# A two-layer decoder trunk on one core: TensorE turns the activations before its last half of a sum, small fp32 products sit in tiles of the array, and ScalarE scales the probabilities

## What is computed

```python
def reference(x, ...):
    for l in range(DEPTH):                       # 2
        x = layer_norm(ALPHA * x + 0.5 * swiglu(x, ffn1_w_gate[l], ffn1_w_up[l], ffn1_w_down[l]), ...)
        mix = hybrid_mixer(x, w_in[l], ...)
        x = layer_norm(ALPHA * x + mix, ln2_g[l], ln2_b[l])
        x = layer_norm(ALPHA * x + 0.5 * swiglu(x, ffn2_w_gate[l], ffn2_w_up[l], ffn2_w_down[l]), ...)

def hybrid_mixer(x, w_in, ...):
    proj = x @ w_in                              # 4864 columns
    b_g, c_g, h, u, q, k, v, gates = split(proj)
    y_conv = short_conv_mixer(b_g, c_g, h, ...) @ w_br_conv
    y_ssm  = s5_mixer(u, ...) @ w_br_ssm         # 16 groups of 16 channels, 64 complex states each
    y_attn = sliding_window_attention(q, k, v, attn_sinks) @ w_br_attn   # 8 heads of 64, window 128
    g = sigmoid(gates)
    return (g[:, :, 0] * y_conv + g[:, :, 1] * y_ssm + g[:, :, 2] * y_attn) @ w_out
```

## Time and profile before

| what | value |
|---|---|
| median of three runs (lowest, highest) | 1177.82 us (1177.39, 1179.10) |
| the profiled execution's own time | 1179.31 us |
| its span | 1177.5 us |
| TensorE busy, weight loads | 97%, 92% |
| VectorE, ScalarE, GpSimd busy | 64%, 49%, 13% |
| mean granted clock of TensorE | 0.991 |

### The profile page before, as it was taken

The page is one execution under the profiler, slowest core; times in us unless marked ns, Lnnn a source line. Parts: engine busy times, 40 slices in busy tenths (PEclk is TensorE's granted clock), DMA queues, the critical chain, the costliest instruction groups (busy, mean ns, idle before and its releaser), DMA issues.

```text
span 1177.5 us, 19863 instructions
## 1 busy us (share of the span) xinstructions
PE 1146.0 (97%) x8174; PEld 1082.3 (92%) x8174; DVE 748.1 (64%) x713; ACT 571.9 (49%) x659; POOL 149.7 (13%) x141
## 2 busy tenths in 40 slices
PE   8999999999999999999999999999999999999996
PEld 7999998999999899999899999979999988999996
DVE  4755447679948674554567554677897585754445
ACT  4655554763443544333356555455734435433441
POOL 1395000003000000000005940000200000000001
PEclk8999999999999999999999999999999999999999
DMA  7765566533465465555546555645435563655550
...
DMA packets 176379, 205.56 MB, mean 175 GB/s; under 512 B 27060, under 2 KB 160840, under 8 KB 176328
## 3 DMA queue, kind: packets, MB, share of 16 engines
...
HBM read 203.77 MB, written 1.05 MB: 174 GB/s over the span
## 4 chain that ended last, share of the span: by engine, by line
PE 83%; DVE 9%; ACT 5%; issue 3%; POOL 0%; POOLq 0%; DVEq 0%; ACTq 0%
PE ps L471 23%; PE ps L442 16%; PE ps L444 16%; PE ps L443 16%; DVE w_lo L1095 3%; ACT w_hi L753 2%; PE ps L455 2%; PE ps L457 1%; PE ps L456 1%; PE ps L717 1%; PE ps L718 1%; PE ps L719 1%; DVE td L1379 1%; DVE bu L1399 1%; DVE tp L1380 1%
## 5 line engine op out<-in xcount | busy, mean ns | idle before, releaser
L1095 DVE TENSOR_TENSOR w_lo<-raw,w_hi 128x2048 fp32r<-128x2048 f32 x185 | 432.3, 2339 | 248.6 <-ACT w_hi L753 248.4
L442 PE MATMUL ps<-xT,w_hi 128*128 128x256 f32 x1856 | 528.3, 285 | 0.9 <-DVE w_lo L1095 0.9
L444 PE MATMUL ps<-xT,w_lo 128*128 128x256 f32 x1856 | 525.2, 283 | 0.0
L443 PE MATMUL ps<-xT,w_hi 128*128 128x256 f32 x1856 | 525.1, 283 | 0.0
L753 ACT CAST w_hi<-raw 128x2048 fp32r<-128x2048 f32 x185 | 351.9, 1903 | 154.2 <-PE ps L444 107.8
L442 PEld LDWEIGHTS ps<-xT,w_hi 128*128 128x128 f32 x1856 | 356.0, 192 | 3.0 <-DVE w_lo L1095 1.3
L443 PEld LDWEIGHTS ps<-xT,w_hi 128*128 128x128 f32 x1856 | 356.1, 192 | 1.7
L444 PEld LDWEIGHTS ps<-xT,w_lo 128*128 128x128 f32 x1856 | 356.0, 192 | 0.0
L471 PE MATMUL ps<-w_hi,rows_hi 128*128 128x512 f32 x416 | 130.8, 391 | 0.3 <-DVE w_lo L1095 0.3
L471 PE MATMUL ps<-w_lo,rows_hi 128*128 128x512 f32 x416 | 130.4, 390 | 0.0
L471 PE MATMUL ps<-w_hi,rows_lo 128*128 128x512 f32 x416 | 130.2, 389 | 0.0
...
## 6 DMA issues: line engine op xcount, KB each, us to landing
...
```

Source lines behind the costliest of these rows:

```text
L442: mm(o, h[:, c, n], xT[:, c, 0, :], start=i == 0, stop=False)
L443: mm(o, h[:, c, n], xT[:, c, 1, :], start=False, stop=False)
L444: last = mm(o, w[:, c, n], xT[:, c, 0, :], start=False, stop=i == KC - 1)
L1095: tt(w_lo[s][:, :], raw[s][:, :], f32(w_hi[s][:, :]), ALU.subtract).then_inc(lo_made.sem, 1)
```

## The change

**Seams.** `transposes` for tile 0 stood behind the last `accumulate`; it now stands ahead of that call's last half (512 columns of tile 1), as `turn()` in `ffn` and written out behind `output(3, ...)`. The sum of tile 0 is finished in two halves that each signal (`acc_done` has three events a norm), and VectorE takes residual and statistics half by half. In the two-chunk seams the turning of tile 1 moved from ahead of the last pair of tile 0 to behind it, and the second chunk's high and low part are made in two halves of four channel blocks (`split_halves`, `rest_halves`), the low halves between the pairs' `x_rest`.

**Start.** The second tile of `x` is loaded behind the first chunk, a copy of one column makes ScalarE load its table early, the first chunk's upper half goes ahead of the cast of the lower blocks, and nine more matmuls on zeros stand behind the first turning.

**Tiles.** The fp32 products name a place in the array: `input_states` a block of 32 rows, the scores one of 64 rows, `output_states` one of 32 columns, `attend` one of 64 columns. Their order alternates between two places. `bTz` and `cTz` shrink to `bT` and `cT`; the clearing of `bTz` (L1341) goes, and the 36 small copies that filled them become five.

**Order in the mixer.** `input_states(0)` comes one chunk earlier, `output_states` later, the steps of the scan stand between low parts, and the probabilities are scaled by 16 ScalarE instructions a layer.

```diff
                 k0 = FFN0[f]
                 if l == 0 and f == 0:
                     load(l, k0, lambda r: [(cols(r)[:, 0:4, :], first[:, 0:4, 0:256])])
+                    sp.dma_start(xtok[:, 1, :], x[0, P:2 * P, :]).then_inc(x_landed[1], 16)
...
-            def gate_up_by_token(l, k0, norm):
-                transposes(l, norm, 0)
+            def gate_up_by_token(l, f, norm):
+                k0 = FFN0[f]
                 take(l, k0)
-                take(l, k0 + 1)
+                pe.wait_ge(second_lo.sem, second_lo.at(l, f))
                 for t in range(NT):
                     part = slice(t * 256, t * 256 + 256)
                     chunks = ((0, ps[:, 0, part], t), (1, ps[:, 1, part], t))
                     for p in range(4):
-                        if t == 0 and p == 3:
-                            transposes(l, norm, 1)
+                        if t == 0 and p == 2:
+                            take(l, k0 + 1)
                         by_token(l, norm, t, p, chunks)
+                    if t == 0:
+                        transposes(l, norm, 1)
...
+                zeros(8)
                 pe.wait_ge(ident_made, 1)
                 transposes(0, -1, 0)
+                zeros(9)
...
                 accumulate(1, 0, tiles=(0,))
                 take(l, k0 + FFN_CHUNKS - 1)
                 pe.wait_ge(h_lo.sem, h_lo.at(l, s0 + STEPS))
-                accumulate(2, 1, stop=True, tiles=(0,)).then_inc(acc_done.sem, 1)
+                accumulate(2, 1, stop=True, tiles=(0,), halves=((0,), (1,))).then_inc(acc_done.sem, 1)
                 accumulate(1, 0, tiles=(1,)).then_inc(used.sem, 1)
-                accumulate(2, 1, stop=True, tiles=(1,), halves=((0,), (1,))).then_inc(used.sem, 1)
+                accumulate(2, 1, stop=True, tiles=(1,), halves=((0,),))
+                turn()
+                accumulate(2, 1, stop=True, tiles=(1,), halves=((1,),)).then_inc(used.sem, 1)
             for l in range(DEPTH):
-                ffn(l, 0, -1)
-                transposes(l, 0, 0)
+                ffn(l, 0, -1, lambda: transposes(l, 0, 0))
...
                 for p in range(4):
                     if q >= 1:
                         pe.wait_ge(bu_made.sem, bu_made.at(l, q))
-                    for t in range(2 * q, 2 * q + 2):
-                        for ri in range(2):
-                            last = mm(ps[:, t % 2, ri * SEQ:ri * SEQ + SEQ], bTz[:, t, ri, :], uT[:, t // 4, :],
-                                      start=True, stop=True)
+                    else:
+                        pe.wait_ge(proj_read.sem, proj_read.at(l, UU + 1))
+                    for ri in range(2):
+                        for t in range(2 * q, 2 * q + 2):
+                            ch = slice(32 * (t % 4), 32 * (t % 4) + 32)
+                            last = mm(ps[:, t % 2, ri * SEQ:ri * SEQ + SEQ], bT[ch, t // 4, ri, :], uT[ch, t // 4, :],
+                                      start=True, stop=True, tile_position=(ch.start, 0))
                     last.then_inc(bu_done.sem, 1)
...
                     pe.wait_ge(x_state_made.sem, x_state_made.at(l, q + 1))
                     ct = q // 2
-                    for t in range(2 * q, 2 * q + 2):
-                        for ri in range(2):
-                            last = mm(ps[:, 2, ct * SEQ:ct * SEQ + SEQ], cTz[:, t, ri, :], sw[:, ri, t % 2, :],
-                                      start=t % 4 == 0 and ri == 0, stop=t % 4 == 3 and ri == 1)
+                    for ri in range(2):
+                        for t in range(2 * q, 2 * q + 2):
+                            ch = slice(32 * (t % 4), 32 * (t % 4) + 32)
+                            last = mm(ps[ch, 2, ct * SEQ:ct * SEQ + SEQ], cT[:, t, ri, :], sw[:, ri, t % 2, :],
+                                      start=ri == 0, stop=ri == 1, skip_group_check=True, tile_position=(0, ch.start))
...
-                        for n, (j, kb) in enumerate(terms):
+                        terms = [(j, kb) for kb in range(blk + 1) for j in range(2)]
+                        for j, kb in terms:
                             head = m + 4 * j
                             i = 2 * head + kb if blk else head
-                            last = mm(ps[:, 3, m * P:m * P + P], vz[:, kb, j, :], probsT[:, i, :],
-                                      start=n == 0, stop=n == len(terms) - 1)
+                            half = slice(HD * j, HD * j + HD)
+                            last = mm(ps[half, 3, m * P:m * P + P], vz[:, kb, j, half], probsT[:, i, :],
+                                      start=kb == 0, stop=kb == blk, skip_group_check=True, tile_position=(0, half.start))
...
-                for head in range(HEADS):
+                by_pairs = [(m + 4 * j, slice(HD * j, HD * j + HD)) for m in range(4) for j in range(2)]
+                for head, half in by_pairs:
                     last = mm(ps[:, head // 2, (head % 2) * SEQ:(head % 2) * SEQ + SEQ],
-                              qT[:, head % 4, P:2 * P], kz[:, head // 4, :], start=True, stop=True)
+                              qT[half, head % 4, P:2 * P], kz[half, head // 4, :], start=True, stop=True,
+                              tile_position=(half.start, 0))
...
                 chunk(CC)
-                chunk(HH)
                 pe.wait_ge(s_made.sem, s_made.at(l, 2))
                 input_states(0)
+                chunk(HH)
                 chunk(BB)
                 chunk(7)
...
                 chunk(10)
-                output_states(1)
                 attend(1)
                 chunk(11)
+                output_states(1)
                 input_states(3)
...
                 chunk(13)
+                output_states(2)
                 chunk(14)
+                chunk(15)
                 output_states(3)
-                chunk(15)
+                chunk(16)
...
-                output(3, (0,)).then_inc(acc_done.sem, 1)
+                output(3, (0,), ((0,), (1,))).then_inc(acc_done.sem, 1)
                 output(2, (1,)).then_inc(used.sem, 1)
-                output(3, (1,), ((0,), (1,))).then_inc(used.sem, 1)
-                ffn(l, 1, 1)
+                output(3, (1,), ((0,),))
+                transposes(l, 1, 0)
+                output(3, (1,), ((1,),)).then_inc(used.sem, 1)
+                ffn(l, 1, 1, lambda: transposes(l, 2, 0) if l < DEPTH - 1 else None)
...
+            def split_halves(l, f):
+                k = FFN0[f] + 1
+                s = k % SLOTS
+                sc_.wait_ge(landed[s], l * LANDED_LAYER[s] + LANDED[k])
+                sc_.wait_ge(used.sem, used.at(l, k - SLOTS + 1))
+                for ks, made in ((slice(4, KC), second_hi), (slice(0, 4), hi_made)):
+                    nc.scalar.copy(cols(w_hi[s])[:, ks, :], cols(raw[s])[:, ks, :]).then_inc(made.sem, 1)
...
+                sc_.wait_ge(zero_made, 1)
+                nc.scalar.copy(warm[:, :], zero_b[:, 0:1])
                 cast(0, 1)
-                cast(0, 0)
                 sc_.wait_ge(first_landed, 16)
                 nc.scalar.copy(cols(w_hi[0])[:, 4:KC, :], cols(raw[0])[:, 4:KC, :]).then_inc(first_hi, 1)
+                cast(0, 0)
                 sc_.wait_ge(landed[0], LANDED[0])
                 nc.scalar.copy(cols(w_hi[0])[:, 0:4, :], cols(raw[0])[:, 0:4, :]).then_inc(hi_made.sem, 1)
...
+                def normalise(S, blk):
+                    for head in range(HEADS):
+                        last = act_(S[:, head, :], S[:, head, :], ACT.Copy, scale=rden[:, blk, head:head + 1])
+                    last.then_inc(probs_made.sem, 1)
...
+                nc.scalar.copy(bT[:, :, :, :], b_ps)
+                cT_ = cT[:, :, :, :].rearrange("p (u q) r n -> p u q r n", u=2)
+                for h in range(2):
+                    half, n = slice(HD * h, HD * h + HD), slice(16 * h, 16 * h + 16)
+                    nc.scalar.copy(cT_[half, :, :, 0, n], c_ps[half, :, 0, :, h, :])
+                    last = nc.scalar.mul(cT_[half, :, :, 1, n], c_ps[half, :, 1, :, h, :], -1.0)
...
                 states(1)
+                sc_.wait_ge(rden_made.sem, rden_made.at(l, 1))
+                normalise(S1, 1)
                 gate(8)
                 split(l, MIX0 + 11)
+                normalise(S0, 0)
                 gate(9)
                 split(l, MIX0 + 12)
                 probs_out(0, 4)
...
-                def normalise(S, blk, n):
-                    tt(S[:, :, :], S[:, :, :], rden[:, blk, :].rearrange("p (h o) -> p h o", o=1)
-                       .to_broadcast([P, HEADS, n]), ALU.mult).then_inc(probs_made.sem, 1)
...
+                def residual_stats(t, h, wait, between=None):
+                    wait()
+                    residual(t, slice(h, h + 1)).then_inc((res_made.sem if h else dve_chain), 1)
+                    if between:
+                        between()
+                    if h:
+                        dve.wait_ge(res_made.sem, res_made.at(l, norm_ * NT + t + 1))
+                    else:
```

(47 more changed lines are left out.)

88 lines of the change are left out of this document (44 added, 44 removed).

## The result

The changed kernel takes 1149.69 us (median of four runs, 1149.53 to 1149.82) against 1178.19 us before; the ratio is 0.9758, with a 95% interval of 0.9741 to 0.9775. The forecast was 1151.0 in a range of 1145 to 1165. The gain of 28.5 us (29.5 us between the two profiled spans, since the profiled execution of before was 1.1 us above its median) lies in case (a), but it is not made up as the sum had it.

What follows compares the result with a forecast made beforehand. TensorE, busy 97% of the span, was taken as the bound. Terms 7.4 + 1.2 + 3.7 + 1.1 + 13.7 - 1.0 = 26.1 us off the 1177.8 median gave 1151.7, stated as 1151, range 1145 to 1165.

Steps and rivals of the forecast that it cites:

- case (a): Whole kernel, the forecast itself: tiles overlap and changes of tiling are cheap, 1147 to 1155 us; chance 0.53.
- FFN seams: Three FFN seams: waits of 2.8 us become 2.05 and the 1.7 us lost to cold clock goes, 7.4 us in all.
- cover most of the chain: FFN seams: six matmuls, 1.4 us, run behind the moved turnings and hide most of a 1.8 us chain, leaving about 0.4.
- K/V seams: Two K/V seams: TensorE waits some 1.0 us, then 0.4, instead of 1.52; gain taken as 0.6 each, 1.2 us.
- Start: Kernel start: first chunk begins at about 8.7 us and chunk 1 at 16.1 instead of 19.86, a gain of 3.7 us.
- Tail: Kernel end: VectorE starts on tile 0's first half 1.4 us earlier, a gain of 1.1 us.
- Tiles: fp32 products in the mixers: overlap saves 18.1 us of 48.2, changes of tiling cost 4.4, net 13.7 us.
- the model of n + 1 steps: Tiled groups: each product's second row runs with the next product's first, so n products take n + 1 steps, not 2n.
- Changes: Borders between whole array and tiles in the mixers: 44 at 0.1 us each, costing 4.4 us.
- 5.8 end: Lower end of the tiles' net gain with overlap, 5.8 us, if each change of tiling costs 0.28 us.
- Mixer's other engines: Mixer: ScalarE's scaling frees 5 us on VectorE, but waits for turned probabilities may grow half a microsecond a layer; minus 1.0 us.
- Case (b): Mixer rival: overlap only in part, as changes of 0.28 us eat it or VectorE's scan binds; 1155 to 1161 us, chance 0.23.

## Why the prediction was right, point by point

- **FFN seams, 7.4 forecast, 6.0 measured** (2.35 + 1.70 + 1.98; the last includes 0.4 lost to a new wait for `hid` in the branches). The mechanism held: pause 1.36 where 1.65 was said, clock full. The step that was mis-sized is "cover most of the chain": at the seam ahead of layer 1 TensorE waits 0.70 us for the normalised tile, since VectorE's residual stands behind a low part there too, which I had seen for the K/V seams only. The clock's part, 5.1 of the 7.4, does not hang on the moved turning: with it moved back the pause is 1.52 us, not 2.72, and the clock stays full. Which of the other edits at the seam (sums, statistics and low parts in halves) shortens the pause no run separates.
- **K/V seams, 1.2 forecast, 0.9 measured.** 0.70 us ahead of the turning and 0.24 behind it, where the text had 1.0 and 0.4; the taken value 0.6 was between the bounds and 0.44 came.
- **Start, 3.7 and 3.3.** First matmul 8.71 (8.7), chunk 1 at 16.60 (16.1); the cast waited 0.31 us for the weights. **Tail, 1.1 and 1.1.**
- **Tiles, 13.7 net forecast, 16.7 by the run without them** (16.2 by its mixers, 133.3 against 125.2 us each). The tiles do run side by side, but both large terms were too small. Overlap, 18.1 in the sum: the model of n + 1 steps let the first row of a group run alone, while the rows start two by two from the first on, and L655, left at nothing, halved as well (0.72 us in each layer). Half of the 48.2 us of rows is 24.1. Changes, 4.4 in the sum (44 at 0.1): 24.1 less the 16.2 that came leaves 7.9; 1.1 of it is TensorE's longer wait for the turned probabilities, and the other 6.8 are 0.15 a change, as the 0.3 to 0.4 us for the way in and out of a group say too. The row that the price was taken from, the 0.20 from 237.37, shows no cost at all: with the 0.03 us ahead of it, it is one step of the 128-column row and one of the chunk. The two errors, 6.0 too little saved and 2.4 too little paid, cancel in part; that each group still came out near the forecast (0.48 and 0.55 us saved where 0.65 less 0.2 for two changes was said) is luck.
- **The rule against the change** in the Trainium skill, TensorEngine Tiling (Array Packing), Key Properties, that a change of mode drains TensorE, would have put the sum at its 5.8 end. The rows agree that a change is not free, 0.3 to 0.4 us for in and out. They also show a group's first weight load at 262.89, together with its matmul, where before it stood 0.12 us ahead of it. But the price is 0.15 to 0.2 a change, not 0.28, and the fuller overlap pays for it.
- **Mixer's other engines, minus 1.0 forecast, at least plus 2.0 measured** (the mixers without tiles are 1.0 shorter each). The wait for probabilities did grow, by about 0.5 a layer, but not because the scaling went to ScalarE: it is 0.7 us in two layers without the tiles, and 1.7 with tiles and the scaling on GpSimd. It is the shorter groups that bring TensorE there earlier. That the scaling's 5 us on VectorE "about pays for" the shorter mixer had the wrong cause: back on GpSimd it costs nothing in the new order. Of the waits for the scan, those at the first outputs are gone with the scaling on ScalarE in the old order and with GpSimd in the new one; the last, 1.65 to 2.3 us a layer, goes with the later `output_states(3)`. The sum named these waits, 0.7 us, but only as a rival, and not what they become with short groups: 6.8 us in the kernel with the tiles alone.

So the total was right within 2 us, while the mixers gave 5.5 us more and the rest 2.1 us less on the span; the mechanism forecast, tiles side by side and a full clock behind the FFN seams, is shown, but the closeness of the sum is partly luck. Case (b), VectorE's scan as the bound, is what would have come without the new order: the stretches of the kernel with the tiles alone (11.4 us off the mixers) and of the changed kernel (11.3 off the rest) give 1155.5, an estimate that no run checks.
